# Expert weights of a two-model kernel: gate and up loaded in quarters of an expert instead of halves

## What is computed

```
def second_block(x, ...):
    h = layer_norm(x, ln_in_g, ln_in_b)
    for i in range(2):
        mix = hybrid_mixer(h, ...)
        h = layer_norm(ALPHA * h + mix, ln1_g[i], ln1_b[i])
        ffn = hierarchical_moe(h, ...)          # 32 experts, each token goes to 2
        h = layer_norm(ALPHA * h + ffn, ln2_g[i], ln2_b[i])

def block_mlp(xb, e):                           # one expert, float32
    h = silu(xb @ w_gate[e]) * (xb @ w_up[e])   # 1024 x 512 each
    return h @ w_down[e]                        # 512 x 1024
```

## Time and profile before

| | |
|---|---|
| median of 3 runs | 1968.52 us (1965.8 to 1970.91) |
| the profiled execution | 1962.59 us |
| its span, first to last instruction | 1960.8 us |
| 824 to 1275 us, most of it the first expert stage | TensorE busy 438.89 of 451 us, 406 GB/s loaded |
| 1493 to 1940 us, most of it the second | TensorE busy 437.02 of 447 us, 409 GB/s loaded |

### The profile page before, as it was taken

How to read it: one execution, slowest core, us unless ns; L and a number is a source line. 1 busy time by engine, 2 the same in 40 slices (tenths; PEclk the granted TensorE clock), 3 DMA queues, 4 the chain that set the end, 5 groups by cost and what they waited for, 6 DMA issues and landing times. The chain is left out here.

```text
span 1960.8 us, 36046 instructions
## 1 busy us (share of the span) xinstructions
PE 1866.0 (95%) x15654; PEld 1278.2 (65%) x15654; DVE 833.2 (42%) x1691; ACT 633.5 (32%) x1209; POOL 53.2 (3%) x58
## 2 busy tenths in 40 slices
PE   7999999899999998899999999999898999999996
PEld 6889998889997887644444434378885444444443
DVE  5767777767775475511111111155734111111112
ACT  4565554565554341211111111143313111111112
POOL 0500000400000000000000000000000000000000
PEclk9999999999999999999999999999999999999999
DMA  7245554245542329399999999743384999999993
GB/s 286 103 148 186 187 194 168 87 151 192 181 165 80 94 92 375 144 406 426 426 426 427 426 427 427 299 124 112 146 360 188 427 426 426 427 426 426 427 427 153
DMA packets 54241, 540.18 MB, mean 275 GB/s; under 512 B 8608, under 2 KB 9536, under 8 KB 16704
## 3 DMA queue, kind: packets, MB, share of 16 engines
q1 hardware_dynamic: 54080, 537.83, 68.1%
HBM read 536.76 MB, written 1.05 MB: 274 GB/s over the span
## 5 line engine op out<-in xcount | busy, mean ns | idle before, releaser
L2873 PE MATMUL experts_psG<-places_gu,experts_xc 128*64 128x512 f32 x1344 | 297.7, 593 | 8.1 <-DMA places_gu<-in_moe_up 8.0
L511 DVE TENSOR_TENSOR ring_low<-ring_raw,ring_high 128x1024 fp32r<-128x1024 f32 x180 | 222.5, 1247 | 99.4 <-ACT ring_high L505 99.3
L2873 PEld LDWEIGHTS experts_psG<-places_gu,experts_xc 128*64 128x64 f32 x1344 | 96.8, 137 | 201.8 <-issue 184.3
L644 PE MATMUL ffn_ps<-first_x_split,ring_high 128*128 128x512 f32 x616 | 220.6, 396 | 0.3
L2803 DVE SCALAR_TENSOR_TENSOR experts_yc_low<-experts_psD,experts_slot_gate,experts_yc_high 128x512 fp32r<-128x512 f32 x64 | 48.0, 750 | 387.9 <-ACT experts_yc_high L2837 387.9
L505 ACT ACTIVATE ring_high<-ring_raw 128x1024 fp32r<-128x1024 f32 x180 | 186.8, 1051 | 70.0 <-PE ffn_ps L646 30.7
L645 PE MATMUL ffn_ps<-first_x_split,ring_low 128*128 128x256 f32 x704 | 183.4, 281 | 0.0
L2793 DVE TENSOR_TENSOR experts_sig<-experts_sig,experts_psG 128x256 f32<-128x256 f32 x64 | 26.9, 421 | 358.2 <-ACT experts_sig L2825 358.2
L2873 PE MATMUL experts_psG<-weights_gu,experts_xc 128*64 128x512 f32 x704 | 156.5, 595 | 3.7 <-DMA weights_gu<-in_moe_up 3.7
L2825 ACT ACTIVATE experts_sig<-experts_psG 128x256 f32<-128x256 f32 x64 | 24.5, 383 | 411.5 <-PE experts_psG L2873 411.5
L645 PEld LDWEIGHTS ffn_ps<-first_x_split,ring_low 128*128 128x128 f32 x704 | 132.1, 188 | 7.1
(11 more groups left out here) (519 smaller groups left out, 3258.4 us busy)
## 6 DMA issues: line engine op xcount, KB each, us to landing
ring_raw<-in_w SPq DMA_DIRECT2D x90, 1024.0 KB, 4.9
places_gu<-in_moe_gate SPq DMA_DIRECT2D x42, 2048.0 KB, 26.9
places_gu<-in_moe_up SPq DMA_DIRECT2D x42, 2048.0 KB, 28.4
places_d<-in_moe_down SPq DMA_DIRECT2D x32, 2048.0 KB, 24.9
weights_gu<-in_moe_gate SPq DMA_DIRECT2D x22, 2048.0 KB, 25.7
weights_gu<-in_moe_up SPq DMA_DIRECT2D x22, 2048.0 KB, 27.2
weights_d<-in_moe_down SPq DMA_DIRECT2D x16, 2048.0 KB, 25.4
experts_d_more<-in_moe_down SPq DMA_DIRECT2D x16, 2048.0 KB, 26.6
```

The lines of the kernel that those rows point to most:

```text
L511: dve.tensor_tensor(self.low[:, n % AHEAD], self.raw_half(n), self.high[:, n % AHEAD], ALU.subtract)\
L644: pe.matmul(out, w[0][:, kk], f.both[:, :, kk], start=kk == 0, stop=False)
L2873: ins = pe.matmul(out, xc[:, kk], wgu[gu[0]][:, kk, :, j * S:(j + 1) * S], start=kk == 0, stop=kk == DT - 1)
```

## The change

The load of a half becomes two loads of a quarter, 1024 KB each, 8 KB to a partition, out of the same rows of device memory (a quarter is every partition's first or second 8 KB of its 16). TensorE counts up `quarter_done` after `kk` = 1, 3 and 5 where it counted up `half_done` after `kk` = 3, and SyncE issues each quarter when the one in its place has been read. Both quarters of a half count on the half's old semaphore, and TensorE still waits at `kk` = 0 and `kk` = 4, now for both. The loads ahead of the stage are in quarters too. Loads of down are as they were.

```
-    def load_half(self, sp, at, place, loaded, half):
-        w = self.gate_up[half]
-        sp.dma_start(self.gu[place][:, half * DT // 2:(half + 1) * DT // 2],
-                     w[bass.ds(at, 1)].rearrange("a p (k g n) -> (a p) k g n", k=DT // 2, g=2))\
-            .then_inc(loaded[place][half], 16)
+    def load_quarter(self, sp, at, place, loaded, q):
+        n = 2 * 2 * EFF
+        w = self.gate_up[q // 2][bass.ds(at, 1), :, (q % 2) * n:(q % 2 + 1) * n]
+        sp.dma_start(self.gu[place][:, 2 * q:2 * q + 2], w.rearrange("a p (k g n) -> (a p) k g n", k=2, g=2))\
+            .then_inc(loaded[place][q // 2], 16)

     def load_gate_up(self, sp, at, place, loaded):
-        for half in range(2):
-            self.load_half(sp, at, place, loaded, half)
+        for q in range(4):
+            self.load_quarter(sp, at, place, loaded, q)
...
-                    sp.wait_ge(half_done, e - (PLACES - 1))
+                    sp.wait_ge(quarter_done, 3 * (e - PLACES) + 1)
                     at = expert(e)
-                    ew.load_half(sp, at, gu[0], gu_loaded, 0)
+                    ew.load_quarter(sp, at, gu[0], gu_loaded, 0)
+                    for q in (1, 2):
+                        sp.wait_ge(quarter_done, 3 * (e - PLACES) + q + 1)
+                        ew.load_quarter(sp, at, gu[0], gu_loaded, q)
                     sp.wait_ge(gu_done, e - (PLACES - 1))
-                    ew.load_half(sp, at, gu[0], gu_loaded, 1)
+                    ew.load_quarter(sp, at, gu[0], gu_loaded, 3)
...
                     for kk in range(DT):
                         if kk % (DT // 2) == 0:
-                            pe.wait_ge(gu_loaded[gu[0]][kk // (DT // 2)], 16 * gu[1] + 16)
+                            pe.wait_ge(gu_loaded[gu[0]][kk // (DT // 2)], 32 * gu[1] + 32)
...
-                        if kk == DT // 2 - 1:
-                            ins.then_inc(half_done, 1)
+                        if kk in (1, 3, 5):
+                            ins.then_inc(quarter_done, 1)
```

More of the change, by code:

```diff
@@ L2701, in stage_experts @@
             d_loaded = [st.sem(f"d_loaded{at}") for at in range(PLACES + 1)]
-        (dve_step, sel_ready, gates_taken, gathered, xc_ready, half_done, gu_done, sig_ready, h_ready, selT_done, selT_ready,
+        (dve_step, sel_ready, gates_taken, gathered, xc_ready, quarter_done, gu_done, sig_ready, h_ready, selT_done, selT_ready,
          hT_done, hT_ready, down_done, gate_ready, yc_rounded, yc_ready, scattered, parts_step, y_done) = [st.sem(s) for s in (
-             "dve_step sel_ready gates_taken gathered xc_ready half_done gu_done sig_ready h_ready selT_done selT_ready "
+             "dve_step sel_ready gates_taken gathered xc_ready quarter_done gu_done sig_ready h_ready selT_done selT_ready "
              "hT_done hT_ready down_done gate_ready yc_rounded yc_ready scattered parts_step y_done").split()]
```

## The result

The changed kernel takes 1975.29 us (median of 6 runs, 1973.37 to 1976.79) beside 1968.84 us for the kernel before in as many runs: ratio 1.004, 95% interval 1.0027 to 1.0052, a loss of 6.45 us.

What follows compares the result with a forecast made beforehand. The prediction took the full DMA stream to bound the expert stages, with TensorE nearly level. Packets +6.9 and earlier starts -1.7 and -0.6 summed to +4.6 us, 1973.1 us on the median, range 1965.5 to 1981.0.

Steps and rivals of the forecast that it cites:

- The bound: In the expert stages the DMA engines are full at a share of 1.01; TensorE waits 5.9 and 5.8 us.
- The end follows the last half: At a stage's end, if the last half lands x later, TensorE ends x later; earlier landing gains up to its waits.
- The last quarter of the first stage: Sign of being right: it lands some 2 us later from the stage's start, and TensorE's waits grow by as much.
- The earlier starts, -1.7 and -0.6 us: At the head of the two stages the first quarter goes out 1.72 us earlier; gain 2.3 us, bounds 0 and 3.4.
- a hole opened before down: Sign of being wrong: at the first stage's head, down lands with a hole in the stream before it.
- The packets, +6.9 us: 116 halves in the stages, packets of 8 KB not 16 KB: 0.059 us a half, from w_out's 1.2% dearer stretch.
- the dearer rival: In the full queue quarters cost over 0.071 us a half; at 0.1 us, +9.3 us, 1977.8, slower; chance 0.30.
- The loads as such at nothing: In the stages' full queue the further loads' starts lie hidden behind other transfers; rival with starts paid: 278 us, chance 0.03.
- SyncE's further issues at nothing: Two more issues per expert on SyncE, 0.33 us each, cost nothing, covered by up to 6.4 us of waiting between issues.
- its line to no change: For the whole kernel's median, 1962.6 to 1974.4 us, about 0.3% or 5.9 us either way, counts as the same.

Runs made afterwards that it cites:

- Without a third of the stream: The kernel before and the changed kernel, each without loads of down from expert 4 on: 1946.30 and 1947.83 us, ratios 0.9896 and 0.9897 to the kernel before.
- late quarters: Changed kernel with its quarters issued two by two where the halves were: 1976.04 us beside 1966.67 for the kernel before, ratio 1.0050.
- expert 3 alone: Kernel before with quarters for expert 3 only, each issued when its place has been read: 1964.20 us beside 1966.67, ratio 0.9984.
- eighths: Changed kernel with each quarter as two loads of 512 KB, rows of 4 KB: 1992.36 us beside 1967.25 for the kernel before, ratio 1.0121.
- long rows and quarters: Kernel before with experts 6 to 19 loaded whole in rows of 32 KB and expert 3 in quarters: 1963.04 us beside 1967.15, ratio 0.9983.

## Why the prediction came out as it did

TensorE's matmuls on the last expert of the first stage, in the kernel before:

```profile
1255.78 7.28 PE L2873 MATMUL experts_psG<-places_gu,experts_xc 128*64 128x512 f32 x32
```

- *The bound.* Right: the engines' share stays at 1.01, and TensorE's waits take up what the stream loses. Without a third of the stream the change shows no price.
- *The end follows the last half.* Right, though thinly, for the first stage before, where TensorE lost 0.24 us at the last half: its matmuls on the last expert took 7.28 us, where they take 7.04 without a wait. Right also for the first stage after, where TensorE waits 1.09 us for the last half. In the second stage after, no wait stands before the last expert. The last wait is the one at 1883 us, four experts earlier, and the slow clock behind it puts TensorE too far back to wait again. The tie is to the latest of several landings near the end, not to the last alone. The last quarter of the first stage was to land some 2 us later after the stage's start, and it landed 3.6 later (1264.6 - 826.49 against 1259.4 - 824.85).
- *The earlier starts, -1.7 and -0.6 us.* The sum of 2.3 agrees with the 2 to 3 us of the late quarters and the 2.5 of expert 3 alone. The parts were 1.1 and 0.8 by down of expert 4: in the first stage a hole opened before down after all, which the prediction had named as a sign of being wrong. Down's landing, at 853.4, came 6.1 us behind the last quarter's at 838.71 + 8.6 = 847.3, where 4.9 is the transfer.
- *The packets, +6.9 us.* The mis-sized term. Rows of 8 KB by themselves cost 8.8 us (6 to 11 by the interval), 0.076 us a half where 0.059 was taken, past the point of 0.071 named for the dearer rival. By the stream alone it is less: 0.94% of twice 430 us is 8.1 us, 0.070 a half, at that point; the interval holds both. The 0.94% falls on the two thirds that are gate and up, so 1.4% on these, where w_out's stretches gave 0.6 and 1.2%. That these came so near is in part luck: by what all queues moved, w_out's two stretches ran at 430 and 426 GB/s, no slower than the stage's 425 to 427, so they show no price by this measure, and they are 4 and 6.5 us long. The engines' share was a poor scale: it runs to 100.7% and, with eighths, 101.6%, so time per MB out of it counts overlaps; MB moved in a full stretch agrees with the time.
- *The loads as such at nothing.* Nearly right: +1.3 us for all further loads (0.2 to 3.9 by the interval). The fixed 2.0 us per transfer that the Trainium skill states ("DMA: Bandwidth & Descriptors", Anatomy of one DMA), for DMAs that GpSimd issues, would be 232 us for 116 loads, an estimate from that page of the Trainium skill. In a full queue, with loads that SyncE issues, the runs do not agree with paying it.
- *SyncE's further issues at nothing.* Right in effect: they take 2.1 us and more late in the stage where 0.33 was taken (last section), and no cost shows.
- *What the sum left out.* TensorE's clock: 1.7 us in the profiled execution, of which an estimated 0.9 added to the time. That the slower stream brought it on is not shown: rows of 16 KB in two loads a half, with the stream as fast as before, had the same fall behind a wait of 2.2 us.

So the case was decided between the forecast and its dearer rival. The mechanism held and the range holds the time, but 1975.29 is past the 1974.4 at which the prediction drew its line to no change: by that line the change is slower, which it gave 0.40, and not the same, which it gave 0.55. The loss is 6.45 us where 4.6 was forecast.

The runs show that shorter rows lower the rate of a full stream; why an engine takes longer for them, no run here shows. The Trainium skill gives a mechanism: "Why small descriptors are slow", on the same page ("DMA: Bandwidth & Descriptors"), counts about 3 cycles per packet beside one per 32 bytes. With one packet to a row that is 0.6% for 8 KB instead of 16 KB, an estimate from that page of the Trainium skill. The runs show the order of row lengths that this asks for and about twice the size, 1.4%; the measurement decides.

## What to carry to other kernels

Where the DMA queue is full, splitting loads for an earlier issue bought only the start of the stage, and each shortening of a partition's row, here from 32 down to 4 KB, lowered the rate for as long as the stream ran: split by partitions, or only the load that starts the stream. Look where the consumer really waits, and lengthen the rows where the stream is still ahead. Price rows by the MB that long full stretches move (100 us here), not by the engines' share.

## What was not expected of the hardware

SyncE stands at its issues when many rows are queued. In the changed kernel:

```profile
1153.23 2.12 SPq L2431 DMA_DIRECT2D places_d<-in_moe_down  x1
1155.40 4.32 SPq L2423 DMA_DIRECT2D places_gu<-in_moe_gate  x2
1159.76 6.78 SPq L2423 DMA_DIRECT2D places_gu<-in_moe_up  x2
```

and with rows of 8 KB in as few loads as before, but not with as many loads of 16 KB rows:

```profile
1149.03 6.79 SPq L2431 DMA_DIRECT2D places_d<-in_moe_down  x1
1155.87 0.54 SPq L2423 DMA_DIRECT2D places_gu<-in_moe_gate  x1
```

```profile
1148.15 1.58 SPq L2425 DMA_DIRECT2D places_gu<-in_moe_gate  x2
1152.84 1.11 SPq L2425 DMA_DIRECT2D places_gu<-in_moe_up  x2
```

So rows count, not loads. By estimate, at 4874 packets in 100 us over 16 engines and some 30 us to landing, about 90 packets stand in an engine's queue when SyncE is held; eighths, with 8451 packets in 100 us and 17.6 us to landing, come to 93. The kernel with 3149 packets in 100 us and 37 us had about 73 and was not held: no single issue there takes over 0.59 us. No cost of it shows here, as the engines stayed full (a share of 1.01).

In five of these kernels TensorE's clock fell after a single wait for a load, of 2.16 to 2.69 us, and the 16 matmuls behind that wait took 5.26 to 5.35 us instead of 3.65; in the changed kernel the clock averages 0.66 from 1883 to 1888 us. It did not fall after waits of 2.22 us in the kernel before (1190 us, clock 1.00 ahead and behind), of 2.14 us with late quarters, and of 2.50 us with long rows and quarters (1203 us, clock 1.00 behind). So the length of the wait alone doesn't decide it; what does was not settled. It is worth up to 1.7 us of a stage between executions.
